# Moving the inverse roots of norms from VectorE's chain to GpSimd's addition and power in a four-layer transformer kernel

## The reference, cut to what matters

```python
def rms_norm(x, g):
    y = x * lax.rsqrt(jnp.mean(x * x, axis=-1, keepdims=True) + EPS)
    return y * g

# 1. border rows: before every layer, over the 1024 columns of a token
h = h + layer(rms_norm(h, norm_g))
# 2. queries and keys: over the 64 or 128 columns of a head
q = rms_norm(q.reshape(..., heads, dim), q_g)
# 3. the output of each head of the differential attention, over 128 columns
o = rms_norm(o, out_g) * (1.0 - lam_init)
```

## Time and profile before

| | |
|---|---|
| times of three runs | 2357.33, 2361.81, 2363.19 us |
| median | 2361.81 us |
| span of the profiled execution, first to last instruction | 2355.0 us |
| TensorE busy | 2248.4 us (95%) |
| VectorE busy | 1377.0 us (58%) |
| ScalarE busy | 1002.5 us (43%) |
| GpSimd busy | 271.0 us (12%), 350 instructions |
| mean granted TensorE clock | 0.988 |

### The profile page before, as it was taken

One profiled execution on the slowest core, in us unless ns is written; L12 is line 12 of the kernel. 1 busy time (PEld: TensorE's weight loads), 2 busy tenths in 40 slices (PEclk: granted clock), 3 DMA queues, 4 the chain that ended last, 5 costly groups with the idle time before them and its releaser, 6 DMA issues. The chain is left out here.

```text
span 2355.0 us, 30828 instructions
## 1 busy us (share of the span) xinstructions
PE 2248.4 (95%) x11479; PEld 1812.9 (77%) x11479; DVE 1377.0 (58%) x2906; ACT 1002.5 (43%) x1896; POOL 271.0 (12%) x350
## 2 busy tenths in 40 slices
PE   5889989899999999999989999999999889999999
PEld 4778767688777777878868788888878658888887
DVE  6976676766656454544584554554455595544643
ACT  5644644433454545453433332233344683322322
POOL 3751000007001010100000000000011230000000
PEclk9999999999999999999999999999999999999999
DMA  7354212124232322224462233322323102323222
GB/s 212 117 170 126 72 54 72 54 89 132 106 109 81 97 73 91 81 77 171 148 220 72 72 95 103 108 80 88 119 72 104 40 2 78 101 90 108 89 92 88
DMA packets 182434, 232.56 MB, mean 99 GB/s; under 512 B 29483, under 2 KB 110850, under 8 KB 182286
## 3 DMA queue, kind: packets, MB, share of 16 engines
q1 hardware_dynamic: 159390, 205.64, 27.2%
q10 hardware_dynamic: 22896, 24.94, 3.3%
HBM read 213.74 MB, written 21.00 MB: 100 GB/s over the span
## 5 line engine op out<-in xcount | busy, mean ns | idle before, releaser
L2094 PE MATMUL G<-w_hi,u_hi 128*128 128x512 f32 x1536 | 621.3, 405 | 7.5 <-issue 5.5
L1629 DVE SCALAR_TENSOR_TENSOR w_lo<-raw,par,w_hi 128x512 fp32r<-128x512 f32 x496 | 370.6, 786 | 423.3 <-ACT w_hi L1094 420.3
L2096 PE MATMUL G<-w_hi,u_lo 128*128 128x512 f32 x1536 | 600.4, 391 | 0.0
L2095 PE MATMUL G<-w_lo,u_hi 128*128 128x512 f32 x1536 | 599.1, 390 | 0.0
L1094 ACT ACTIVATE w_hi<-raw,par 128x512 fp32r<-128x512 f32 x496 | 317.5, 715 | 375.6 <-PE G L2096 362.3
L2094 PE MATMUL G<-u_hi,w_hi 128*128 128x512 f32 (+1 forms) x1168 | 460.9, 395 | 11.8 <-DVE u_lo L1695 11.8
L2096 PE MATMUL G<-u_hi,w_lo 128*128 128x512 f32 (+1 forms) x1168 | 448.6, 384 | 0.0
L2095 PE MATMUL G<-u_lo,w_hi 128*128 128x512 f32 (+1 forms) x1168 | 448.5, 384 | 0.0
L2094 PEld LDWEIGHTS G<-w_hi,u_hi 128*128 128x128 f32 x1536 | 288.9, 188 | 73.9 <-issue 13.1
L2096 PEld LDWEIGHTS G<-w_hi,u_lo 128*128 128x128 f32 x1536 | 288.6, 188 | 62.3
L2095 PEld LDWEIGHTS G<-w_lo,u_hi 128*128 128x128 f32 x1536 | 289.3, 188 | 59.7 <-issue 1.9
(11 more groups left out here) (307 smaller groups left out, 2341.1 us busy)
## 6 DMA issues: line engine op xcount, KB each, us to landing
raw<-in_ffn_w_up SPq DMA_DIRECT2D x88, 512.0 KB, 4.8
raw<-in_e_w_in SPq DMA_DIRECT2D x56, 512.0 KB, 4.7
raw<-in_o_w_in SPq DMA_DIRECT2D x56, 512.0 KB, 4.5
raw<-in_ffn_w_down SPq DMA_DIRECT2D x40, 512.0 KB, 4.3
raw<-in_e_w_out SPq DMA_DIRECT2D x16, 512.0 KB, 4.6
raw<-in_o_w_out SPq DMA_DIRECT2D x16, 512.0 KB, 4.2
raw<-in_a_w_glu SPq DMA_DIRECT2D x16, 512.0 KB, 4.7
raw<-in_w_kv SPq DMA_DIRECT2D x16, 512.0 KB, 4.3
```

The lines of the kernel that those rows point to most:

```text
L1629: V.scalar_tensor_tensor(w_lo[:, n % HL, k], raw[:, n % RAW, k], gain(name, k0 + k), w_hi[:, n % HL, k].bitcast(F32), ALU.mult, ALU.subtract)\
L2094: pe.matmul(out, lh, rh, start=start, stop=False)
L2095: pe.matmul(out, lh, rl, start=False, stop=False)
L2096: return pe.matmul(out, ll, rh, start=False, stop=stop)
```

## The change

The inverse root of a sum of squares is formed on GpSimd by two instructions, an addition of the epsilon (or of the two halves' sums) and a power with the exponent -0.5, where VectorE ran its chain of shift, integer step and three rounds. VectorE waits for the result and scales as before. This holds for the border rows (`pool_h_rms`, one column at a time), for the sixteen chunks of queries and keys (`pool_q_rms`, all columns in one instruction) and for the heads of the differential attention (`pool_o_rms`, four columns). The epsilon of the first column part of a border is added on GpSimd as well. GpSimd takes these pieces at fixed places of its queue: a head's root between the second and third square of a chunk where one is due. The scaling of a head moves from slot t-4 to slot t-5, behind that slot's scores and weights. The mean's factor is folded into the gains, whose number of instructions stays six. The memory's rows, the first layer's rows and the first two chunks are left on VectorE.

```diff
+        minus_half = small[:, 61:62]
...
+                mark("h_rms", s.i, t)
                 mark("xn_ready", s.i, t)
...
             prev.tail = state["lead"] = s
+            tails.append((prev.n + prev.nu - 1, s))
...
+            if q.squares == "q_squared":
+                mark("q_rms", q.i)
...
                     mark("o_squared", s.i, hd)
+                    mark("o_summed", s.i, hd)
+                    mark("o_rms", s.i, hd)
                     mark("on_ready", s.i, hd)
...
                 before, at = attention("A", 4, 4 * g, len(plan)), 7
+                a_mixes.append(before)
...
+            def pool_h_rms(s):
+
+                pool.wait_ge(*at_("h_squared", s.i, 0, TT - 1))
+                do(pool.tensor_scalar(ss[:, 0:TT], ss[:, 0:TT], EPS, None, ALU.add))
+                for t in range(TT):
+                    pool.wait_ge(*at_("h_squared", s.i, 1, t))
+                    v = ss[:, TT + t:TT + t + 1]
+                    do(pool.tensor_tensor(v, v, ss[:, t:t + 1], ALU.add))
+                    pool.tensor_tensor(rstd[:, t:t + 1], v, minus_half, ALU.pow).then_inc(*by("h_rms", s.i, t))
+
+            def pool_o_rms(s, hd):
+
+                pool.wait_ge(*at_("o_summed", s.i, hd))
+                do(pool.tensor_scalar(oss, oss, P * EPS, None, ALU.add))
+                pool.tensor_tensor(orstd, oss, minus_half.to_broadcast([P, TT]), ALU.pow)\
+                    .then_inc(*by("o_rms", s.i, hd))
+
+            def pool_q_rms(q):
+
+                N = q.T * 512 // q.hd
+                pool.wait_ge(*at_("summed", q.i, q.T - 1))
+                do(pool.tensor_scalar(qk_ss[:, 0:N], qk_ss[:, 0:N], q.hd * EPS, None, ALU.add))
+                pool.tensor_tensor(qk_rstd[:, 0:N], qk_ss[:, 0:N], minus_half.to_broadcast([P, N]), ALU.pow)\
+                    .then_inc(*by("q_rms", q.i))
...
+            do(pool.memset(minus_half, -0.5))
...
+                heads = [(s, n - s.n - 2) for s in a_mixes if 0 <= n - s.n - 2 < s.heads]
                 for k, s in enumerate(qk_chunks):
                     if s.n + 2 == n and k > 1:
                         for m in range(s.T):
+                            if m == 2 and heads:
+                                pool_o_rms(*heads.pop())
                             x = att[:, 12 + s.stage_at + m, :]
...
+                if heads:
+                    pool_o_rms(*heads.pop())
...
+                for s in qk_chunks:
+                    if s.n + s.nu == n and s.squares == "q_squared":
+                        pool_q_rms(s)
+                for last, s in tails:
+                    if n == last:
+                        pool_h_rms(s)
...
             def finish_rms(q):
+                if q.squares == "q_squared":
+                    dve.wait_ge(*at_("q_rms", q.i))
+                    return
                 dve.wait_ge(*at_("summed", q.i, q.T - 1))
...
             def rms_tiles(s, ts):
 
                 for t in ts:
-                    dve.wait_ge(*at_("h_squared", s.i, 1, t))
-                    step(t, V.tensor_tensor(col(lnv, t), col(ss, 4 + t), col(ss, t), ALU.add))
...
-                for _ in range(3):
...
-                for t in ts:
-                    dve.wait_ge(chain["dve"], last[t])
-                    V.tensor_scalar(xn_view[:, t, :], h[:, t, :], col(rstd, t), None, ALU.mult)
+                    dve.wait_ge(*at_("h_rms", s.i, t))
+                    V.tensor_scalar(xn_view[:, t, :], h[:, t, :], rstd[:, t:t + 1], None, ALU.mult)\
+                        .then_inc(*by("xn_ready", s.i, t))
...
                 if m == 0:
-                    dve.wait_ge(*at_("h_squared", s.i, 0, TT - 1))
-                    link("dve", dve, V.tensor_scalar(ss[:, 0:4], ss[:, 0:4], EPS, None, ALU.add))
                     rms_tiles(s, (0,))
...
                         dve.wait_ge(*at_("o_squared", s.i, hd))
-                        link("dve", dve, V.tensor_reduce(oss, on, AX_X, ALU.add))
-                        inverse_rms(orstd, oss, P, oln)
-                        dve.wait_ge(*at_("o_copied", s.i, hd))
-                        V.tensor_tensor(on, o_copy.rearrange("p (a b) -> p a b", b=P),
-                                        orstd.unsqueeze(2).to_broadcast([P, TT, P]), ALU.mult)\
-                            .then_inc(*by("on_ready", s.i, hd))
+                        V.tensor_reduce(oss, on, AX_X, ALU.add).then_inc(*by("o_summed", s.i, hd))
...
+                if is_last(s, t - VALUE - 1) and s.akind == "A":
+                    hd = s.steps[t - VALUE - 1][0]
+                    dve.wait_ge(*at_("o_rms", s.i, hd))
+                    dve.wait_ge(*at_("o_copied", s.i, hd))
+                    V.tensor_tensor(junk[:, 0, :].rearrange("p (a b) -> p a b", b=P),
+                                    o_copy.rearrange("p (a b) -> p a b", b=P),
+                                    orstd.unsqueeze(2).to_broadcast([P, TT, P]), ALU.mult)\
+                        .then_inc(*by("on_ready", s.i, hd))
...
-                for name, f in (("aq", 64 ** -0.5), ("cq", P ** -0.5), ("exq", P ** -0.5), ("oxq", P ** -0.5),
-                                ("sq", 64 ** -0.5), ("aout", 1.0 - LAM_INIT)):
+                for name, f in (("exq", P ** -0.5), ("ak", 64 ** 0.5), ("ck", P ** 0.5), ("oxk", P ** 0.5),
+                                ("sk", 64 ** 0.5), ("aout", (1.0 - LAM_INIT) * P ** 0.5)):
```

More of the change, by code:

```diff
@@ L245, in build @@
         state = dict(n=0, norm=0, chunk=0)
+        tails, a_mixes = [], []
         def aux(*key, ready=True):
@@ L1652, in rms_tiles @@
             def rms_tiles(s, ts):
[L1654 to L1662, removed]
-                for t in ts:
-                    dve.wait_ge(*at_("h_squared", s.i, 1, t))
-                    step(t, V.tensor_tensor(col(lnv, t), col(ss, 4 + t), col(ss, t), ALU.add))
-                for t in ts:
-                    dve.wait_ge(chain["dve"], last[t])
-                    step(t, V.tensor_scalar(col(rstd, 4 + t).bitcast(I32), col(lnv, t).bitcast(I32), 1, None,
-                                            ALU.logical_shift_right))
-                for t in ts:
-                    step(t, V.tensor_scalar(col(lnv, 4 + t), col(lnv, t), -0.5, None, ALU.mult))
-                    dve.wait_ge(chain["dve"], last[t])
-                for t in ts:
-                    step(t, V.tensor_scalar(col(rstd, t).bitcast(I32), col(rstd, 4 + t).bitcast(I32), -1.0,
-                                            float(0x5f3759df), ALU.mult, ALU.add))
-                for _ in range(3):
-                    for t in ts:
-                        dve.wait_ge(chain["dve"], last[t])
-                        y = col(rstd, t)
-                        step(t, V.scalar_tensor_tensor(col(rstd, 4 + t), y, y, col(lnv, 4 + t), ALU.mult, ALU.mult))
-                    for t in ts:
-                        dve.wait_ge(chain["dve"], last[t])
-                        y = col(rstd, t)
-                        step(t, V.scalar_tensor_tensor(y, col(rstd, 4 + t), 1.5, y, ALU.add, ALU.mult))
-                for t in ts:
-                    dve.wait_ge(chain["dve"], last[t])
-                    V.tensor_scalar(xn_view[:, t, :], h[:, t, :], col(rstd, t), None, ALU.mult)                        .then_inc(*by("xn_ready", s.i, t))
+                for t in ts:
+                    dve.wait_ge(*at_("h_rms", s.i, t))
+                    V.tensor_scalar(xn_view[:, t, :], h[:, t, :], rstd[:, t:t + 1], None, ALU.mult)\
+                        .then_inc(*by("xn_ready", s.i, t))
             def u_low(s, t):
```

## The result

Over four runs each, the changed kernel takes 2339.44 us (2335.96 to 2341.57) and the one before 2360.16 us (2357.33 to 2363.19). The ratio is 0.9913, with a 95% interval of 0.9901 to 0.9925. Forecast were 2341.5 us. The kernel is faster by 0.9%, which is more than the 0.3% that can be told from no change.

What follows compares the result with a forecast made beforehand. TensorE, busy 95% of the span, was taken as the bound, so only its waits and lower clock could yield time. 8.8 + 7.2 + 1.9 + 2.4 = 20.3 us off 2361.8 gave 2341.5 us, own range 2335 to 2348.

Steps and rivals of the forecast that it cites:

- Borders: At five layer borders, two root chains in a row before the split get shorter, 1.76 us each: 8.8 us.
- Heads: In the differential attention, VectorE without the chain is less late for scores and gating: 7.2 us over the heads.
- Queries and keys: Sixteen chunks: 1.9 us at the odd layer's memory chunk, where TensorE waited; the other fifteen have cover, counted at nothing.
- Clock: After shorter waits TensorE regains a third of the 7.4 us lost at its lower clock behind borders: 2.4 us.
- The price x: Time of a border root on GpSimd with handovers, addition 0.3 and power 0.6: 1.2 us.
- a cap of about 2.0: Limit in us on the gain at the two borders with short waits, where 1.76 just uses them up.
- rival D: A head's root between squares delays the third and fourth square and holds VectorE up: 3 to 5 us, 2346; chance 0.06.
- the replay: VectorE's queue at a head, without chain and scaled a slot later: 1.35 us of 2.84 waiting remains at head 0.
- One of the signs: In the queries' and keys' chunks, the scaling L1649 waiting for GpSimd would make the prediction wrong.
- A: The power is slow, each microsecond costing 10 us over five borders: about 2362 to 2373 us; chance 0.14.
- C: The power is middling, 1.2 to 2 us, so borders gain 2.8 or lose 5: 2350 to 2358 us; chance 0.15.
- B: The later slot eats the heads' gain, each of eight heads waiting 1.1 us more for scaling: 2360 us; chance 0.07.

Runs made afterwards that it cites:

- doubling the power: The changed kernel with a second, unused one-column power before each border root's power; 2344.01 us, ratio 0.9945.
- the multiplication: The changed kernel with a multiplication of two constants in place of each border root's power, so border roots aren't computed; 2337.59 us, ratio 0.9909.
- the squares first: The changed kernel, but GpSimd takes all four squares of a chunk ahead of a head's root, not two; 2336.18 us, ratio 0.9897.
- the old slot: The changed kernel, but a head is scaled one slot earlier, where it was before the change; 2343.01 us, ratio 0.9924.
- the heads alone: The changed kernel, but borders, queries and keys keep VectorE's chain; only heads have GpSimd roots and the later slot; 2352.95 us, ratio 0.9964.

## Why the prediction was right, step by step

The forecast held, and most of its mechanisms did. That it came within 2 us is in part luck. The sum of 20.3 us stands beside 20.7 in medians, but beside 17.8 in the two profiled executions from which the terms can be read, and in these the borders were 1.5 too low while heads and clock were 1.5 and 1.7 too high. This is how the terms came out. Clock steps are in a line of their own.

| Term | Forecast | Measured |
|---|---|---|
| Borders | 8.8 | 10.3 |
| Heads | 7.2 | 5.7 |
| Queries and keys | 1.9 | 1.7 |
| Clock | 2.4 | 0.7 |
| Small shifts elsewhere | 0 | -0.6 |
| Sum | 20.3 | 17.8 |

**Borders.** That two roots lie in a row and the other two are covered was right; doubling the power showed it. The price x was 1.02 us and not 1.2: the addition took 0.19 and not 0.3 (one column is cheaper than the 32 columns of the earlier trace rows), the power 0.63 and not 0.6. Border 4, where no clock step is in the difference, gained 2.07, and five times that are 10.3. Of the two short borders, for which the prediction put a cap of about 2.0, only border 4 has one: the multiplication brings it to about 2.3 and no further. Border 1 goes on: its 0.74 more make some 2.8. The waits for u_lo fell to 7.5 and not to 4 or 5, because only 4.8 us of the gain came off them. 2.9 came off the "issue" waits (5.5 to 2.6) and 1.7 off those of the turns for the scaled rows.

**Heads.** I take the table's rows, add back one clock step of 1.6 at head 2, and take off the 1.1 us that heads 1 to 3 of the second group owe to the clock: their row is -2.8, but TensorE's idle time there fell by only 1.7 (6.8 to 5.1), and the mean granted clock rose from 0.88 to 0.91. Head 0 gained 1.9 each time (forecast 1.5), head 1 of the first group 2.1 (3.1), heads 1 to 3 of the second 1.7 (1.8 and part of the 0.4), head 3 of the first 0.4. Head 2 lost 2.3 where 1.1 were forecast. What failed there is the weight given to rival D: the replay left out that the displaced squares run beside VectorE's weights. With the squares first the loss is 0.92, and the 1.1 were right. At head 1 of the first group the replay left 1.35 us of waiting, and 2.55 are there. Two squares run beside the weights and the scaling in the changed kernel there as well:

```profile
317.70 1.29 POOL L1103 TENSOR_TENSOR work<-att 128x512 f32<-128x512 f32 x1
319.27 1.17 POOL L1103 TENSOR_TENSOR work<-att 128x512 f32<-128x512 f32 x1 [0.28 <-ACT att L1150]
...
318.13 1.41 DVE L1812 SCALAR_TENSOR_TENSOR big<-big,small 128x512 f32<-128x512 f32 x1
319.47 1.52 DVE L1833 TENSOR_TENSOR work<-big,small 128x512 f32<-128x512 f32 x1
...
321.04 0.66 PE L2207 MATMUL X<-ident,work 128*128 128x128 f32 x4 [2.55 <-DVE work L1833]
```

Before, these two instructions took 0.75 and 0.69 us, so they are 1.5 longer. Putting the squares first doesn't move these two, and the wait stays; that they are its cause is read from the trace and not tested. That the remaining wait stands before the scaled head was right in kind, but the 8 us given for it were too low: 12.9 were measured. The replay's own terms, 1.35 three times, 4.0 and 1.9, already add up to 10.

**Queries and keys.** The 1.7 at oxq came. "The remaining fifteen are counted at nothing" was right for the time of the changed kernel, but nearly wrong: the prediction asked for a takeover of over 6 us before anything was late, and it is 6.55. One of the signs that would make the prediction wrong did appear: L1698, its L1649, waits for GpSimd in twelve chunks, 45.1 us in all. The sign was badly chosen, since it watches an engine that isn't the bound; TensorE's waits for that scaling fell from 4.3 to 2.6 us. The cover turned out as 7.95, since GpSimd may start earlier than VectorE's chain did, ahead of the split. Alone, this part costs at least as much as it brings.

**The clock.** This is the step that failed. It took for granted that shorter waits only give clock back. At the borders 4.4 us came back, in three of five, and 1.1 at the second group's heads. But a step also came where the wait had grown (head 2), and two came in stretches without an edit: 4.8 us in all. What decides whether a step comes isn't settled, nor is it at the borders. Behind the same wait border 2 keeps its step in the changed kernel and with the squares first, and loses it with the old slot; and border 1 loses its step with the heads alone too, where the border is as before. So the 4.4 are measured, but that shorter waits brought them isn't shown. The step at 130-150 appears in the changed kernel, and in four of the twelve variants, with the same code around it.

**The rivals.** A and C, the slow and the middling power, fell with 0.63 us for a column. Their slope of 10 us per microsecond was right: 0.6 us more cost about 6 in the borders. The prediction set GpSimd's 0.30 us for 32 columns against VectorE's 0.16 for one. At one column both, it is 0.19 to 0.16, so a plain instruction of this size is far from twice as slow on GpSimd. The warning in A about the 32 columns, 0.2 us a column, was close, at 0.165. B, the later slot eating the gain, isn't what happened, and the reverse is shown: without the later slot the heads bring 0.5. D happened at one head, for 1.4 us, and at a second squares slow VectorE down by 1.5. What the four rivals missed is that queries and keys could be the part without worth.

## What to carry to other kernels

When a chain moves to an engine with free time, add up the new engine's duration against the first consumer's slack for each width in use: the same power was a gain at one column and none at 32, where doubling it cost 56 us. Work taken off an engine that is not the bound, as VectorE's 2.4 us of chain per chunk, is worth nothing where that engine then waits for the result. A part that is moved and a slot that is moved for it belong together and are tried both ways; here the root alone was worth about nothing, and the slot alone cost some 15 us.

## What was not expected of the hardware

- The power on GpSimd grows almost linearly with its columns: 0.63, 1.07, 2.00, 3.25 and 5.73 us for 1, 4, 8, 16 and 32 columns of 128 partitions.
- A GpSimd addition of one column takes 0.19 us. But its TENSOR_SCALAR on four columns took 0.23 us at head 0 in the variant with the old slot, where VectorE waited, and 0.94 at the same head in the changed kernel, where VectorE ran a split:

```profile
295.57 0.74 DVE L1675 SCALAR_TENSOR_TENSOR w_lo<-raw,par,w_hi 128x512 fp32r<-128x512 f32 x1
...
295.75 0.94 POOL L1052 TENSOR_SCALAR small<-small 128x4 f32<-128x4 f32 x1 [52.47 <-DVE small L1823]
```

- It also goes the other way: VectorE's single column took 0.80 us beside a square of GpSimd and 0.16 without, and the scaling of a head took 1.52 in place of 0.69.
- A clock step costs TensorE about 1.6 us, and it comes and goes between variants in stretches that they don't edit. In differences of a few microseconds it is as large as the effects themselves, so a single span doesn't decide between them.
